# Two heads' scores at every second step, and a new order for ScalarE and VectorE at the odd steps, in layer A of a four-layer fp32 kernel

## The reference, cut to what matters

```
h = rms(x);  q, k, v, g = split(h @ w_in)          # each 1024 wide
q, k = rope(rms(q per 64)), rope(rms(k per 64))    # per head two halves c = 0, 1 of 64
s_c = q_c k_c^T / 8, causal                        # 256 x 256, per head and half
a   = softmax(s_0) - lam * softmax(s_1)
o   = rms(a @ v) * silu(g);   x = x + o @ w_out
```

## Time and profile before

| what | value |
|---|---|
| median of 3 runs | 948.66 us (948.6 to 948.98) |
| the profiled execution | 950.42 us, its span 948.7 us |
| TensorE busy in the span | 936.5 us (99%) |
| VectorE, ScalarE busy | 756.8 us (80%), 623.8 us (66%) |
| mean granted TensorE clock | 0.999 |

### The profile page before, as it was taken

How to read it: one execution, slowest core, us unless ns; L and a number is a source line. 1 busy time by engine, 2 the same in 40 slices (tenths; PEclk the granted TensorE clock), 3 DMA queues, 4 the chain that set the end, 5 groups by cost and what they waited for, 6 DMA issues and landing times.

```text
span 948.7 us, 17189 instructions
## 1 busy us (share of the span) xinstructions
PE 936.5 (99%) x6988; PEld 813.6 (86%) x6988; DVE 756.8 (80%) x1214; ACT 623.8 (66%) x1046; POOL 15.5 (2%) x28
## 2 busy tenths in 40 slices
PE   9999999999999999999999999999999999999997
PEld 7878789988889987889888888899888888888886
DVE  5787678555867998787999888877877779988885
ACT  6666767347766775577766666777456777666664
POOL 0000000000000000000000000004000000000000
PEclk9999999999999999999999999999999999999999
DMA  8734454743254444354676665645545637766651
GB/s 304 255 115 148 142 165 143 228 145 120 89 178 115 153 120 128 90 182 133 196 226 218 188 191 180 198 135 155 158 121 166 204 114 214 214 207 186 198 189 55
DMA packets 44654, 158.07 MB, mean 167 GB/s; under 512 B 4896, under 2 KB 6432, under 8 KB 44576
## 3 DMA queue, kind: packets, MB, share of 16 engines
q1 hardware_dynamic: 43568, 154.29, 52.5%
q0 software_dynamic: 576, 2.10, 0.6%
q10 hardware_dynamic: 432, 0.59, 0.2%
HBM read 155.91 MB, written 1.05 MB: 165 GB/s over the span
## 4 chain that ended last, share of the span: by engine, by line
PE 90%; ACT 4%; DVE 4%; DMA 1%; issue 0%; ACTq 0%; DVEq 0%
PE psum L433 88%; PE psum L442 2%; DVE w_lo L411 1%; ACT w_hi L398 1%; DMA raw<-in_pieces 1%; ACT scr L3158 0%; ACT normed L574 0%; DVE scr L3168 0%; DVE scr L3476 0%; ACT u_both L2980 0%; DVE scr L3150 0%; DVE scr L3144 0%; ACT L3268 0%; DVE feat L3470 0%; ACT scr L3453 0%
## 5 line engine op out<-in xcount | busy, mean ns | idle before, releaser
L411 DVE TENSOR_TENSOR w_lo<-raw,w_hi 128x1024 fp32r<-128x1024 f32 x241 | 290.9, 1219 | 43.1 <-ACT w_hi L398 42.6
L398 ACT ACTIVATE w_hi<-raw 128x1024 fp32r<-128x1024 f32 x241 | 249.8, 1052 | 41.7 <-PE psum L433 32.6
L433 PE MATMUL psum<-w_hi,u_hi 128*128 128x512 f32 x336 | 135.5, 404 | 0.6 <-ACT w_hi L784 0.3
L433 PE MATMUL psum<-w_hi,u_lo 128*128 128x512 f32 x336 | 130.9, 391 | 0.0
L433 PE MATMUL psum<-u_both,w_hi 128*128 128x512 f32 (+1 forms) x544 | 125.6, 378 | 0.0
L433 PEld LDWEIGHTS psum<-u_both,w_hi 128*128 128x128 f32 x544 | 97.6, 188 | 19.8 <-ACT w_hi L398 1.6
L433 PE MATMUL psum<-w_lo,u_hi 128*128 128x512 f32 x336 | 103.8, 390 | 0.0
L433 PE MATMUL psum<-u_hi,w_hi 128*128 128x256 f32 x320 | 81.7, 288 | 0.0
L433 PE MATMUL psum<-u_lo,w_hi 128*128 128x256 f32 x320 | 80.0, 283 | 0.0
L433 PEld LDWEIGHTS psum<-w_hi,u_hi 128*128 128x128 f32 x336 | 63.1, 188 | 15.4 <-issue 2.5
L3168 DVE SCALAR_TENSOR_TENSOR scr<-scr,cols 128x255 f32<-128x255 f32 (+1 forms) x176 | 73.5, 478 | 2.5 <-ACT scr L3158 2.3
(11 more groups left out here) (338 smaller groups left out, 1593.4 us busy)
## 6 DMA issues: line engine op xcount, KB each, us to landing
raw<-in_pieces SPq DMA_DIRECT2D x287, 512.0 KB, 3.8
post_gain<-in_norm_gains POOLq DMA_DIRECT2D x4, 512.0 KB, 4.0
x_res<-in_x SPq DMA_DIRECT2D x4, 256.0 KB, 5.6
const<-in_table SPq DMA_DIRECT2D x1, 928.0 KB, 6.6
out_x<-x_res SPq DMA_DIRECT2D x1, 512.0 KB, 2.6
cols<-in_cols SPq DMA_DIRECT2D x1, 384.0 KB, 6.5
raw<-in_pieces ACTq DMA_DIRECT2D x1, 256.0 KB, 5.0
raw<-in_pieces SPq DMA_DIRECT2D x1, 256.0 KB, 4.7
```

The source lines that it names most:

```text
L398: act.q.activation(w_hi[slot[i]][:, :], raw[i % RAW][:, :], ACT.Copy).then_inc(act.done, act.mark("hi", i))
L411: dve.q.tensor_tensor(w_lo[slot[i]][:, :], raw[i % RAW][:, :], w_hi[slot[i]][:, :].bitcast(F32), ALU.subtract).then_inc(dve.done, dve.mark ...
L433: return pe.q.matmul(o, lhs, rhs, start=start, stop=stop, **kw)
```

## The change

TensorE's `pe_a_scores` takes a pair of heads and is called at the even steps 0, 2, 4 and 6 alone: first the masks of both heads, then the tile matmuls of the one and of the other. At the odd steps TensorE has no scores. On ScalarE the exponentials of an odd head go ahead of `act_a_quarter(2 * step + 1)`, that is ahead of the piece's copy and of the bank's move; at even steps nothing changes. On VectorE the maxima of an odd head go ahead of the mix of the head before.

```
-    def pe_a_scores(h):
-        sc = sets[h % 2]
-        for c in (0, 1) if h < 4 else (2, 3):
+    def pe_a_scores(heads):
+        rows = [slice(64 * c, 64 * c + 64) for c in range(2)]
+        for c in (0, 1) if heads[0] < 4 else (2, 3):
             pe.wait_ge(act, "A.qkT", c)
             pe.wait_ge(dve, "A.qkT", c)
         pe.wait_ge(act, "A.causal")
-        if h >= 2:
-            pe.wait_ge(act, "A.probs", h - 2)
-        for c in range(2):
-            mask_diagonal(sc[:, c, 0:384], ident_r, causal_r)
-        rows = [slice(64 * c, 64 * c + 64) for c in range(2)]
...
+        for h in heads:
+            if h >= 2:
+                pe.wait_ge(act, "A.probs", h - 2)
+            for c in range(2):
+                mask_diagonal(sets[h % 2][:, c, 0:384], ident_r, causal_r)
+        for h in heads:
+            sc = sets[h % 2]
...
         for step in range(DA_HEADS + 2):
-            if step < DA_HEADS:
-                pe_a_scores(step)
+            if step < DA_HEADS and step % 2 == 0:
+                pe_a_scores((step, step + 1))
...
+            if step < DA_HEADS and step % 2:
+                act_a_probs(step)
             if step < 9:
                 act_a_quarter(2 * step + 1)
...
-            if step < DA_HEADS:
+            if step < DA_HEADS and step % 2 == 0:
                 act_a_probs(step)
             if step < 9:
                 act_a_quarter(2 * step + 2)
...
+            if step < DA_HEADS and step % 2:
+                dve_a_peak(step)
             if 1 <= step <= DA_HEADS:
                 dve_a_mixed(step - 1)
-            if step < DA_HEADS:
+            if step < DA_HEADS and step % 2 == 0:
                 dve_a_peak(step)
```

More of the change, by code:

```diff
@@ L1018, in pe_a_scores @@
         pe.wait_ge(act, "A.causal")
-        if h >= 2:
-            pe.wait_ge(act, "A.probs", h - 2)
-        for c in range(2):
-            mask_diagonal(sc[:, c, 0:384], ident_r, causal_r)
-        rows = [slice(64 * c, 64 * c + 64) for c in range(2)]
[L1024 to L1030, removed]
+        for h in heads:
[5 more added lines that the diff above has]
+            sc = sets[h % 2]
+            for g in (0, 64):
+                for c, r in enumerate(rows):
+                    mm(sc[g:g + 64, c, 0:P], qt[r, h, g:g + 64], kt[r, h, 0:P], False, False, True)
+            for g in (0, 64):
+                for c, r in enumerate(rows):
+                    last = mm(sc[g:g + 64, c, P:3 * P], qt[r, h, P + g:P + g + 64], kt[r, h, 0:S], False, True, True)
+            last.then_inc(pe.done, pe.mark("A.scores", h))
     def pe_a_mixed(h):
```

## The result

The changed kernel takes 965.79 us (median of four executions, 963.82 to 966.53), the kernel before 948.82 us beside it: ratio 1.0171, 95% interval 1.0159 to 1.0183, 17 us slower. The direction and the mechanism are those of the prediction; the size lies above its range. The profiled execution is the fastest of the four, with a span of 962.5 us.

A forecast was written before the change was run, and what follows sets the result against it. TensorE was taken as the bound, busy 61.00 of 61.00 us in steps 0 to 7. Stalls 3.1 + 3.4 + 1.6 + 4.2 = 12.3, less 1.3 saved, add 11.0 to 948.66: 959.7 us, range 956.0 to 964.0.

The forecast's parts named there:

- The chain at the odd steps: Steps 1, 3, 5, 7: maxima, exponentials and piece copy delay ScalarE's move; TensorE stalls 3.1, 3.4, 1.6, 4.2 us.
- The additional table loads: ScalarE's step 7, around head 7's exponentials: two loads of 1.28 us; rival without extra loads: 957.1 us, chance 0.10.
- a drain: Rival at ScalarE's step 7: each table switch also drains, two loads 2.7 us dearer, 962.5 us; chance 0.03.
- The pairs' saving: TensorE's scores: second head costs 0.87 instead of 1.14 us; 0.3 saved a pair, 1.3 taken for four pairs.
- The edits costed at nothing: VectorE's later mixes, pair scores needing two earlier heads' exponentials, and late piece copies: taken to cost nothing.
- the missing cover: ScalarE works two pieces ahead of TensorE; without that, a piece would cost what the bank's move costs now.
- The clock falls: Rival: after 3-4 us stalls TensorE gets 1.2 GHz for one or two quarters; 962.4 to 965.2 us, chance 0.17.
- the sum: At quarter 16: stalls of 12.3 less 1.3 saved, 11.0 us later; nothing added or returned from step 8 on.
- rows 2: Profile rows of steps 0 to 7 before the change: TensorE busy 61.00 of 61.00 us, clock 1.00.
- The base of the sum: Profiled execution's 950.42 would be 961.4; carried to the median of 948.66, span the same within a tenth, 959.7 us.

The follow-up runs named there:

- the kernel with the move first: The changed kernel, but at odd steps ScalarE's bank move goes ahead of the exponentials, the piece's copy behind them; 951.01 us, ratio 1.0017 to the kernel before.
- the filled kernel: The changed kernel plus 13, 13, 6 and 18 unread mask matmuls on TensorE in the four waits; 961.83 us, ratio 1.0132 to the kernel before.
- the second profile of the changed kernel: The changed kernel run once more, nothing altered; 966.25 us against 949.26 for the kernel before, ratio 1.0176.
- the pairs alone: The kernel before with only TensorE's paired scores, ScalarE's and VectorE's orders as before; 948.22 us against 949.18, ratio 0.9989.

## Why the prediction was right, and where it was wrong

**The chain at the odd steps: right.** Maxima from 54.70, exponentials from 55.95, the move's end at 59.56: these stand in the profile as they stand in the prediction. The waits were 3.1, 3.4, 1.6 and 4.2, and are 3.23, 3.29, 1.65 and 4.47. Taking ScalarE's order back removes them, and it alone brings them; shortening what stands ahead of the move by a copy or a table load shortens them by that much.

**The additional table loads: right.** There are two of 1.28 us each. The exponentials begin 0.01 us behind the load's end (110.02 + 1.28 to 111.31). The Trainium skill (ScalarE: Activation LUTs, "What ACT_TABLE_LOAD costs") gives a drain of 1.38 us on top; the trace leaves no room for it here either, and the wait at quarter 16 came out within 0.3 us of the sum without it.

**The pairs' saving: right in kind, too large.** 1.3 was worked out and 1.0 measured. I counted 0.05 to 0.10 a pair for the first instruction behind the tiles, besides the 0.27 by which the second head is cheaper; only about 0.26 a pair came on average. The second head's tile matmuls cost what was worked out: 0.65 (1.46 less 0.81).

**The edits costed at nothing: right where they were used.** VectorE's order cost nothing. That ScalarE's two pieces of advance cover the late copies held in the changed kernel, since TensorE was late itself. Without that lateness it fails at step 7, as the prediction's own sentence on the missing cover said: the kernel with the move first waits 1.4 us there by the list. That features too stand behind the exponentials (0.5 us at step 4 there) is not in the prediction.

**The clock: the step that failed.** The prediction had "The clock falls" as a rival, with 0.17, at the price of one or two slow quarters of 2.7 us, and put nothing for it into the sum. It is a term: with the waits filled it is gone, and 4.3 us with it. In the two profiles it fell behind two waits (2.8 us) and behind three (5.2), so at 1.4 and 1.7 us each. The forecast was 6.1 us short. Besides the 4.3, the waits less the pairs are 0.9 above the sum (11.9 by the filled kernel against 11.0); for the remaining microsecond the loss at 677 to 702 us is likely and not shown. With the clock as a term, 11.0 plus the 2.8 to 5.2 of the two profiles, the time would have been 962.5 to 964.9; the 965.8 measured lie close above.

What the rival rested on, a clock of 1.00 behind a wait of 1.2 us, says nothing of waits of 3 to 4 us, and three of these were forecast in the same text. Moreover rows 2 end at 106 us, ahead of that wait (116.9 to 118.0). The row that covers it does show 1.00, as does the next one up to 140 us:

```profile
106.00:120.00 14.00, 12.83 (x71) 10.71 (x70) 10.58 (x18) 10.96 (x23) 0.00 (x0) 1.00 0.40 121
```

And it is not so that no row of before shows the lower clock within the span. In the last 2.4 us of it the clock is at 0.50, when TensorE is idle after its last matmul (start 943.37):

```profile
946.30:948.70 2.40, 0.00 (x0) 0.00 (x0) 0.25 (x1) 0.00 (x0) 0.00 (x0) 0.50 0.58 219
```

So the trace of before held a fall of the clock, 2.9 us behind the start of the last matmul, and the forecast waits could have been held against it. The Trainium skill's rule (TensorE: Matmul & The Clock Gate, Part 1), that TensorE is given the lower clock when it has been idle, was the better guide, and the traces agree with it: 0.50 behind five of the six waits of over 3 us in the two profiles of the changed kernel, 1.00 behind both of 1.65 us.

**The base of the sum.** The prediction says that the span of the median execution is that of the profiled one within a tenth; no span of the median execution is on record. In the executions of before that ran later the span is 1.3 to 1.8 us under the time, which would put it at about 947 for 948.66. The forecast does not hang on it, since 11.0 was added to the time.

**What stays open.** Why the same wait of 3.2 us at quarter 4 is followed by a fall in one execution and not in another. It is not the wait's length, which is the same to 0.01 us. And why TensorE loses up to a microsecond at 677 to 702 us in some executions, in a part of the kernel that no edit touched.

## What to carry to other kernels

When a step is moved ahead on an engine that serves the bottleneck, list what it now stands in front of, and ask for each whether the bottleneck waits for it at once: here the 0.69 us move out of a bank that was to be reused in half a microsecond. Work that is ready, or that frees a buffer, goes ahead of work that still waits for something; the same rule found 1.2 us in a place that the change had not touched. And when waits of several microseconds are forecast for TensorE, put the clock behind them into the sum.

## What the runs showed of the hardware

In all profiles together the clock did not fall behind waits of 1.6 to 1.7 us or less; it fell behind one of two waits of 2.3, behind seven of nine of 3.0 to 3.3, and behind all six of 3.5 and more (by matmul starts). Matmuls whose results nobody reads, issued to fill the waits, kept it at 1.00. The low stretch can begin while TensorE is at work again: 1.5 us after its return at step 1 of the second profile of the changed kernel. The tile matmuls of two heads run through without a pause between them: 1.46 us for 32 (46.39 to 47.85, the pairs alone), where 16 took 0.81 (67.81 to 68.62).
